# Decoder layer on one core: the w_down product in two halves of 1024 columns, with seven block products for 8 of the 22 pairs of k tiles in each

## What is computed

```
h = rmsnorm(x, g_ffn_pre[l])
ff = (jax.nn.silu(h @ w_gate[l]) * (h @ w_up[l])) @ w_down[l]
x = x + rmsnorm(ff, g_ffn_post[l])
```

## Time and profile before

| | |
|---|---|
| time, median of 3 runs | 1215.16 us (1214.73 to 1216.29) |
| the profiled execution's own time | 1216.34 us |
| its span, first to last instruction | 1214.6 us |
| mean granted TensorE clock | 0.998 |
| PE busy | 1202.1 us, 99% |
| DVE, ACT, POOL busy | 857.3, 651.6, 153.6 us |
| chain that ended last | PE 94%, DMA 3%, DVE 2%, ACT 1% |
| loads of w_down | 44 of 1 MB |

### The profile page before, as it was taken

The page is one execution under the profiler, slowest core; times in us unless marked ns, Lnnn a source line. Parts: engine busy times, 40 slices in busy tenths (PEclk is TensorE's granted clock), DMA queues, the critical chain, the costliest instruction groups (busy, mean ns, idle before and its releaser), DMA issues.

```text
span 1214.6 us, 16282 instructions
## 1 busy us (share of the span) xinstructions
PE 1202.1 (99%) x5812; PEld 1007.3 (83%) x5812; DVE 857.3 (71%) x1107; ACT 651.6 (54%) x860; POOL 153.6 (13%) x122
## 2 busy tenths in 40 slices
PE   8999999999999999999999999999999999999997
PEld 7888888888888888888888888888888888888886
DVE  6657877877776755777888888788888744444444
ACT  5654666474564745655555555555555544343432
POOL 2000200000000000004333323432332100000000
PEclk9999999999999999999999999999999999999999
DMA  8656867767686555464566556566555755555651
GB/s 314 210 148 159 208 152 160 176 138 209 159 198 189 193 206 180 168 193 155 206 208 207 189 184 216 172 207 207 197 187 187 259 207 181 201 192 189 205 176 69
DMA packets 121842, 229.60 MB, mean 189 GB/s; under 512 B 7360, under 2 KB 24000, under 8 KB 121280
## 3 DMA queue, kind: packets, MB, share of 16 engines
q1 hardware_dynamic: 121504, 226.85, 60.1%
q0 software_dynamic: 288, 2.10, 0.4%
HBM read 226.83 MB, written 2.10 MB: 188 GB/s over the span
## 4 chain that ended last, share of the span: by engine, by line
PE 94%; DMA 3%; DVE 2%; ACT 1%; issue 0%; SPq 0%; DVEq 0%; ACTq 0%
PE bank L1580 92%; DMA raw<-in_w_in 2%; PE bank L1878 1%; DMA resid<-in_x 1%; DVE w_lo L1002 1%; ACT w_hi L603 0%; PE bank L1585 0%; PE bank L1794 0%; DVE h L1029 0%; DVE resid L1344 0%; PE bank L1851 0%; DVE hT L1015 0%; DVE gT L1229 0%; ACT L771 0%; DVE ff_out L1337 0%
## 5 line engine op out<-in xcount | busy, mean ns | idle before, releaser
L1580 PE MATMUL bank<-w_hi,h2T 128*128 128x512 f32 x1126 | 359.4, 390 | 0.0
L1002 DVE TENSOR_TENSOR w_lo<-raw,w_hi 128x1024 fp32r<-128x1024 f32 x172 | 209.3, 1223 | 129.9 <-ACT w_hi L603 129.3
L603 ACT ACTIVATE w_hi<-raw 128x1024 fp32r<-128x1024 f32 x172 | 180.6, 1059 | 174.3 <-PE bank L1580 159.4
L1580 PE MATMUL bank<-hT,w_hi 128*128 128x512 f32 x768 | 271.7, 397 | 0.0
L1580 PEld LDWEIGHTS bank<-w_hi,h2T 128*128 128x128 f32 x1126 | 211.3, 188 | 44.0
L1580 PE MATMUL bank<-w_hi,ffT 128*128 128x512 f32 x704 | 217.2, 389 | 0.0
L1580 PE MATMUL bank<-hT,w_lo 128*128 128x256 f32 x768 | 214.6, 279 | 0.0
L1580 PE MATMUL bank<-w_lo,h2T 128*128 128x512 f32 x543 | 211.4, 389 | 0.0
L1544 DVE TENSOR_TENSOR w_lo<-raw,w_hi 128x1024 fp32r<-128x1024 f32 x88 | 107.9, 1226 | 121.3 <-ACT w_hi L963 121.3
L1481 DVE TENSOR_TENSOR w_lo<-raw,w_hi 128x1024 fp32r<-128x1024 f32 x116 | 148.3, 1285 | 47.6 <-ACT w_hi L927 47.3
L1580 PEld LDWEIGHTS bank<-hT,w_hi 128*128 128x128 f32 x768 | 144.0, 187 | 32.4
(11 more groups left out here) (212 smaller groups left out, 1217.4 us busy)
## 6 DMA issues: line engine op xcount, KB each, us to landing
raw<-in_w_in SPq DMA_DIRECT2D x63, 1024.0 KB, 10.0
raw<-in_w_down SPq DMA_DIRECT2D x44, 1024.0 KB, 5.0
raw<-in_w_up SPq DMA_DIRECT2D x80, 512.0 KB, 4.0
raw<-in_w_gate SPq DMA_DIRECT2D x80, 512.0 KB, 4.8
raw<-in_w_out SPq DMA_DIRECT2D x16, 1024.0 KB, 5.0
raw<-in_w_gate SPq DMA_DIRECT2D x4, 1024.0 KB, 5.2
raw<-in_w_up SPq DMA_DIRECT2D x4, 1024.0 KB, 6.4
resid<-in_x SPq DMA_DIRECT2D x2, 1024.0 KB, 7.2
```

The source lines that it names most:

```text
L603: act.activation(part_of(w_hi, rnd, s), src, ACT.Copy).then_inc(hi_done, 1)
L1002: dve.tensor_tensor(part_of(w_lo, rnd, s), raw_sub(rnd, s)[1], part_of(w_hi, rnd, s).bitcast(F32), ALU.subtract).then_inc(lo_done, 1)
L1580: return pe.matmul(out_, lhsT, rhs, start=start, stop=stop, skip_group_check=True)
```

## The change

**w_down by halves.** Columns 0 to 1023 are one group, 1024 to 2047 another. In each, 22 units of two k tiles, a chunk of 512 + 512 columns of w_down, loaded as two transfers of 512 KB with the code of the gate and up groups. `DOWN` gives the kinds: units 2, 4, ... 16 by seven products, the others regular, so S and R units alternate and five R units stand at the end. `unit_hi`, `unit_lo`, `weight_sums`, `partial_sums`, `up_sums` and `gate_sums` are used for both kinds of group. The half's sums go to `down_part`, from which squares and gains are taken; `ff_out` shrinks to the first half's columns. In the second half the last eight pieces are reordered so that the first 512 columns are complete before the last four pieces, which are done tile by tile as before.

**Sums of ff pair by pair.** The tokens' block sums of ffT (`token_sums`) are made for each S unit anew, 16 times: POOL adds hi and lo (128 x 512) and makes four sums of 128 x 128, between its first and its second difference of that unit; behind the unit's second piece ACT rounds them (128 x 512) and DVE makes their rest (128 x 512) into `d_ops`, which has two places. PE waits for that (`d_ready`) before the unit's first piece.

The core of the diff:

```diff
 FINAL = Plan("RRSRSRRR")
+DOWN = Plan("RRSRSRSRSRSRSRSRSRRRRR")
+LAST_HALF = Plan(DOWN.units)
+LAST_HALF.pieces[-8:] = [(n, piece) for piece in range(2) for n in range(18, 22)]
+DOWN_SEVEN = [n for n in range(KF // 2) if DOWN.units[n] == "S"]
 DOWN_FIRST = FF_FIRST + (FF_GROUPS - 2) * FULL.subs + FINAL.subs
-R_DOWN = R_FF + 2 * FF_GROUPS
-DOWN_SUBS = KF // 2
-N_SUBS = DOWN_FIRST + 4 * DOWN_SUBS
+N_SUBS = DOWN_FIRST + 2 * DOWN.subs
...
+def chunk_of(i, n):
+
+    return (n if down_half(i) is None else KF // 2 * down_half(i) + n) % 4
...
-        ff_out = sb("ff_out", [P, TT, D], stack=last)
+        ff_out = sb("ff_out", [P, TT, D // 2], stack=last)
         g_post2 = sb("g_post2", [P, D], stack=last)
+        down_part = sb("down_part", [P, 4, 512], stack=last)
+        d_ops = sb("d_ops", [P, 2, 2, 4, P], F32R, stack=last)
+        d_whole = sb("d_whole", [P, 2, SEQ], stack=last)
+        d_sum = sb("d_sum", [P, 4, P], stack=last)
...
-            for n in range(4 * KF // 4):
-                g, k = divmod(n, KF // 4)
-                load(R_DOWN + n // 4, n % 4, rows(w_down, 4 * k, 4, 512 * g, 512),
-                     counted=DOWN_FIRST + 8 * (n // 4))
+            ends = [ff_base(FF_GROUPS - 1) + FINAL.base[n + 1] for n in range(4, 8)]
+            for half, (up_col, gate_col) in enumerate(((512, 0), (1024, 1536))):
+                i = FF_GROUPS + half
+                ends += [ff_base(i) + DOWN.base[n + 1] for n in range(KF // 2)]
+                for n in range(KF // 2):
+                    unit_rows(i, n, ends[KF // 2 * half + n], ((w_down, up_col), (w_down, gate_col)))
...
+            def weight_sums(i, n, plan, between=None):
+
+                q, made = chunk_of(i, n), sums_index(i, n)
+                b12, b22, b11, b21 = (raw[:, q, 512 * c:512 * (c + 1)] for c in range(4))
+                pool.wait_ge(raw_up[q], up_arrived(i, n))
                 pool.tensor_tensor(b12, b22, b12, ALU.subtract).then_inc(t3_ready, 1)
-                pool.wait_ge(t2_ready, 3 * i + (j - 2))
+                if between:
+                    between()
+                pool.wait_ge(t2_ready, made + 1)
                 pool.tensor_tensor(b22, b22, b11, ALU.subtract).then_inc(t14_ready, 1)
-                pool.wait_ge(lo_done, ff_base(i) + (FULL.base[n] + 2))
+                pool.wait_ge(lo_done, ff_base(i) + (plan.base[n] + 2))
                 pool.tensor_tensor(b21, b21, b11, ALU.subtract).then_inc(t14_ready, 1)
...
+            def token_sums(d, n):
+
+                a11, a21 = d_whole[:, 0, 0:P], d_whole[:, 0, P:SEQ]
+                a12, a22 = d_whole[:, 1, 0:P], d_whole[:, 1, P:SEQ]
+                if d:
+                    pool.wait_ge(d_step, 5 * d)
+                    pool.wait_ge(d_ready, d)
+                pool.tensor_tensor(d_whole[:], ffT[:, 2 * n:2 * n + 2, 0:SEQ].bitcast(F32),
+                                   ffT[:, 2 * n:2 * n + 2, SEQ:2 * SEQ].bitcast(F32), ALU.add).then_inc(d_step, 1)
+                pool.wait_ge(d_step, 5 * d + 1)
+                pool.tensor_tensor(d_sum[:, 0], a21, a22, ALU.add).then_inc(d_step, 1)
+                pool.tensor_tensor(d_sum[:, 2], a11, a21, ALU.subtract).then_inc(d_step, 1)
+                pool.wait_ge(d_step, 5 * d + 2)
+                pool.tensor_tensor(d_sum[:, 1], d_sum[:, 0], a11, ALU.subtract).then_inc(d_step, 1)
+                pool.wait_ge(d_step, 5 * d + 4)
+                pool.tensor_tensor(d_sum[:, 3], a12, d_sum[:, 1], ALU.subtract).then_inc(d_step, 1)
+
+            pool.wait_ge(ff_lo, 2 * FF_GROUPS - 2)
+            for half in range(2):
+                for c, n in enumerate(DOWN_SEVEN):
+                    d = len(DOWN_SEVEN) * half + c
+                    weight_sums(FF_GROUPS + half, n, DOWN, between=lambda: token_sums(d, n))
...
+                    if plan.units[n] == "S" and piece == 1:
+                        d = len(DOWN_SEVEN) * half + DOWN_SEVEN.index(n)
+                        act.wait_ge(d_step, 5 * d + 5)
+                        act.activation(d_ops[:, d % 2, 0], d_sum[:], ACT.Copy).then_inc(d_rounded, 1)
...
+                    if plan.units[n] == "S" and piece == 1:
+                        d = len(DOWN_SEVEN) * half + DOWN_SEVEN.index(n)
+                        dve.wait_ge(d_rounded, d + 1)
+                        dve.tensor_tensor(d_ops[:, d % 2, 1], d_sum[:], d_ops[:, d % 2, 0].bitcast(F32),
+                                          ALU.subtract).then_inc(d_ready, 1)
...
+                    if m in (6, 8) and half == 1:
+                        if m == 6:
                             dve.wait_ge(post_in, 32)
-                        emptied(2 + g % 2, ff_out, g_post2, g, Q_POST2)
+                        gained(i - 1, m // 8, m // 8)
+                    if half == 1 and m == plan.subs - 4:
+                        partial_sums(i, DOWN, 4)
+
...
+                if t == 0:
+                    dve.wait_ge(tile_full, 2)
+                else:
+                    dve.wait_ge(sub_done, N_SUBS)
+                gate_sum_of(FF_GROUPS + 1, t, 0)
+                dve.wait_ge(sq_done, Q_POST2 + TT * 3 + t + 1)
+                link(dve.tensor_tensor(down_part[:, 2 * t, :], down_part[:, 2 * t, :], g_post2[:, 1536:D], ALU.mult))
...
+                if half is None:
+                    j = SEVEN.index(n)
+                    s1, s2, s3, s4 = ((s_upper(j)[:, c, :], s_lower(j)[c // 2][:, c % 2, :]) for c in range(4))
+                else:
+                    d = len(DOWN_SEVEN) * half + DOWN_SEVEN.index(n)
+                    s1, s2, s3, s4 = ((d_ops[:, d % 2, 0, c, :], d_ops[:, d % 2, 1, c, :]) for c in range(4))
+                    if piece == 0:
+                        pe.wait_ge(d_ready, d + 1)
+                pe.wait_ge(lo_done, ff_base(i) + (m + 1))
+                if first and piece == 2:
+                    pe.wait_ge(ff_lo, 2 * i if half != 1 else 2 * FF_GROUPS)
+                pair = (((c0 + 2, s4, False), (s0 + 2, tokens(0, 0), first)), ((c0, tokens(0, 1), False),),
+                        ((s0, s3, first), (s0 + 3, s2, first)),
+                        ((s0 + 1, s1, first), (c0 + 1, tokens(1, 1), False)))[piece]
+                for c, (b, operand, new_) in enumerate(pair):
+                    ins = products(b, *operand, slot, c, new_)
+                ins.then_inc(sub_done, 1)
...
-            pe.wait_ge(part_done, 2 * FF_GROUPS - 2)
-            for g in range(4):
-                pe.wait_ge(acc_free, E_DOWN + g + 1)
-                for s in range(DOWN_SUBS if g < 3 else DOWN_SUBS - AHEAD):
-                    n = DOWN_SUBS * g + s
-                    if g == 0:
-                        pe.wait_ge(ff_lo, s + 1)
-                    sub_tokens(DOWN_FIRST + n + 1, down_slot(n), ffT, 2 + g % 2, 2 * s, KF - 1)
-                    if g == 0 and s == 1:
-                        turned_ff(FF_GROUPS - 1, 0)
-            last_subs(DOWN_FIRST + 3 * DOWN_SUBS, DOWN_SUBS - AHEAD, DOWN_SUBS, ffT, 3)
+            def down_group(half, plan):
+
+                i, odd = FF_GROUPS + half, half == 0
+                c0, s0 = sum_banks(odd)
+                pe.wait_ge(part_done, 2 * i - 2)
+                for m in range(plan.subs - 4 * half):
+                    n, piece = plan.pieces[m]
+                    if plan.units[n] == "R":
+                        if n == KF // 2 - 4:
+                            pe.wait_ge(ff_lo, 2 * FF_GROUPS)
+                        sub_tokens(ff_base(i) + (m + 1), ff_slot(i, odd, m), ffT, c0 // 2 + 1 - piece, 2 * n, KF - 1)
+                        if m == 2 and half == 0:
+                            turned_ff(i - 1, s0)
+                    else:
+                        if n == DOWN_SEVEN[0] and piece == 0:
+                            pe.wait_ge(gate_sum, 2 * i - 2)
+                        seven_piece(i, odd, plan, m, c0, s0)
+
+            down_group(0, DOWN)
+            down_group(1, LAST_HALF)
```

More of the change, by code:

```diff
@@ L260, in hybrid_layer, with parts, ff @@
         ctx.callback(ffn.close)
-        def ff(t):
-            return part[:, 2 * t + 1, :]
+        def parts(i):
+            return part if down_half(i) is None else down_part
+        def ff(t, i=0):
+            return parts(i)[:, 2 * t + 1, :]
         def s_upper(j):
@@ L334, in hybrid_layer @@
         s_summed = sem("s_summed")
+        d_step = sem("d_step")
+        d_rounded = sem("d_rounded")
+        d_ready = sem("d_ready")
         s_rounded = sem("s_rounded")
@@ L932, in first_product @@
                 act.wait_ge(sub_done, ff_base(i) + plan.after_seven)
-                act.activation(part[:, 0, :], bank[:, s0 + 2, :], ACT.Copy).then_inc(p1_out, 1)
+                act.activation(parts(i)[:, 0, :], bank[:, s0 + 2, :], ACT.Copy).then_inc(p1_out, 1)
             def ff_group(i, odd, plan=FULL, first=False):
@@ L955, in _ @@
             ff_group(FF_GROUPS - 1, False, FINAL)
[L958 to L973, removed]
@@ L974, in _, with square_dump @@
-            for g in range(4):
[L975 to L978, removed]
```

(40 more changed lines are left out.)

210 lines of the change are left out of this document (115 added, 95 removed).

## The result

| | before | changed |
|---|---|---|
| median | 1215.13 us (4 runs, 1214.73 to 1216.29) | 1243.62 us (4 runs, 1243.03 to 1248.17) |
| ratio | 1 | 1.0232 [1.0213, 1.0251] |
| the profiled execution: time, span | 1216.34, 1214.6 us | 1243.03, 1241.3 us |
| mean granted TensorE clock | 0.998 | 0.999 |

A forecast was written before the change was run, and what follows sets the result against it. The prediction took the turn shared by DVE and POOL in the w_down stage as the bound: -10.9 + 51.8 + 1.0 + 2.4 + 0.7 = +45.0 us on the median 1215.2 gives 1260 us, range 1240 to 1284.

The forecast's parts named there:

- the full turn: w_down stage: DVE's and POOL's SBUF operations, served one after the other, set the pace; 1251 to 1281 us, chance 0.74.
- Matmuls removed: w_down stage: 16 S units save 3 matmuls each, 48 x 0.2267 = -10.9 us, if PE is fed.
- The turn's first signs in the gate groups: Gate groups: ACT waits 20.8 us for POOL's L577, PE loses 3.0 us to a late `w_lo`.
- DVE and POOL take turns: S and R units: DVE operations with two SBUF inputs and POOL's are served one after the other, 10.45 us per pair.
- The length of a step, 13.9: w_down, S unit to S unit: 13.9 us against PE's 10.20, 3.7 us of waits in fourteen steps, +51.8 us.
- First S unit +1: First half of w_down: the first S unit's pieces come 0.3 to 1.5 us late, priced +1 us.
- gain products +2.4: Second half of w_down: the first half's four gain products stand among the S units, 4 x 0.61 = +2.4 us.
- The end, +0.7: Kernel's end: the last result needs DVE's addition from PSUM before ACT's square, +0.7 us.
- Priced at nothing: w_down stage: partial sums, ACT's rounding of token sums, loads and added waits were taken to add nothing to the sum.
- B, PE fed: Rival, w_down stage: PE stays fed if the turn is below 10.9 us a step; 1205 us, chance 0.08.
- C, half of it: Rival, w_down steps: POOL's short operations slip in beside DVE's or the ring covers more; 1233 us, chance 0.10.
- D: Rival, w_down steps: the chain of waits from POOL's dependent sums adds to the turn; 16.9 us a step, about 1300, chance 0.08.

## Why the prediction was right, and where its size was off

It named the sign, the mechanism and the place. Its forecast of 1260 was 16.4 us over the 1243.62 measured, which lies inside its range. But its lowest case for the full turn, 13.4 us a step and 1251 us, was above what came: the time is inside only because the range reached down to 1240. By its steps:

- **Matmuls removed, -10.9.** Right: 5764 for 5812, at the distance of before.
- **The turn's first signs in the gate groups.** One of them was misread: the 3.0 us for a late `w_lo` in the earlier trace rows are the idle time of PEld, the weight loads. PE itself lost nothing there; it was busy for 264.98 of 265.00 us. The sum doesn't use it.
- **DVE and POOL take turns.** Right, and shown: with fills in place of POOL's reads the step is 10.9, with the sums running unhooked it is unchanged.
- **The length of a step, 13.9, measured 12.93.** This is the term of the sum that was mis-sized. Two of its parts are measured by themselves. The step without POOL's sums, 10.45 + 0.61 = 11.06, is 10.90: 0.16 too much. POOL's sums, 1.24 + 1.6 = 2.84, are 2.03: 0.81 too much. In the turn a 512-column operation holds 2.27 - 1.14 = 1.13 and not 1.24, and a short one 1.42 - 1.14 = 0.28 and not 0.4, as the chain of the changed kernel shows in steady alternation (start, us, what):

```profile
1010.39 1.42 POOL d_sum L643
```

  By these holds the five sums would be 2.25, 0.2 more than the 2.03. Most of that is at the last sum, L645, which meets a short DVE operation: from DVE's sum L1570 to its next operation it is 0.76 us (1011.51 to 1012.27), and 0.61 in the kernel with the sums made once, so only 0.15 is added. The start of an operation, which I had added to each of them, seems to lie beside DVE's operation: 0.28 and less are held, where a short one alone takes 0.46. So PE waits 2.73 a step and not 3.7: 14 x 0.97 = 13.6 of the 16.4 us.
- **First S unit +1, gain products +2.4.** Together 38.7 - 14 x 2.73 = 0.5 us where 3.4 was forecast. The first S unit does lose 0.61 and 0.58 us, at 979.49 and 981.72, and the gains do stand in the turn (two operations of 0.61 take 3.49):

```profile
1109.66 3.49 DVE L1629 TENSOR_TENSOR ff_out<-down_part,g_post 128x512 f32<-128x512 f32 x2
```

  I had counted both on top of full steps. PE's timeline shows otherwise. From the first matmul with `d_ops` of one S unit to that of the next, the first step is 12.43 us in the first half (976.67 to 989.10) and 13.14 in the second (1109.88 to 1123.02), and each of the other twelve is 12.93 to 12.95. So the first S unit's loss lies inside a first step that is 0.5 shorter than the others. The second half's first step, which has the four gain products, is 0.7 longer than the first half's, where 2.4 was priced. That PE starts these steps with four pieces ready in the ring is my explanation; no run tests it.
- **The end, +0.7.** Right: 0.74, also with all units regular. In DVE's timeline:

```profile
1233.19 0.69 DVE L1509 TENSOR_TENSOR down_part<-down_part,bank 128x512 f32<-128x512 f32 x1 [0.23 <-PE bank L1692]
```

- **Priced at nothing: partial sums, ACT's rounding, smaller loads, the added waits.** Right. The loads: the stage is 240.06 with all units regular. The added waits: the unhooked sums. The partial sums: PE waits for nothing from 1066.72 to 1113, which covers the start of the second half. The rounding: DVE stands for it once, for 0.2 us.
- **Rivals.** B, PE fed: its condition, a step of 10.9 as the point of break-even, was met by the two kernels without POOL's reads, and they broke even. With two R units to an S unit and POOL held back PE is fed, and the kernel is 6.2 us faster, with 36 matmuls removed that are worth 8.2. C, half of it: 14 x 2.73 = 38.2 of the 51.8 showed, because short operations take their turn but hold it shortly, not because they slip in beside DVE's. D: excluded, by the unhooked sums.

The rule cited there from the Trainium skill (SBUF — State Buffer, Who interferes with whom), that the loser is blocked for the whole instruction, agrees with the short operations here: 1.32 to 1.44 us for 128 columns beside a 1024-column operation of DVE, against 0.46 where DVE reads a PSUM bank, as here in POOL's timeline:

```profile
1094.24 0.46 POOL L641 TENSOR_TENSOR d_sum<-d_whole 128x128 f32<-128x128 f32 x1
```

That 0.46 is near the 0.41 I estimated from GPSIMD Engine Reference, section Elementwise — side-by-side cycle accounting, and the estimate of 0.28 from its 2.6 cycles for each element alone is the most that such an operation holds of the turn (0.15 to 0.28).

## What to carry to other kernels

- Where DVE operations with two SBUF inputs meet POOL operations that read SBUF, add the two per step and compare the sum with PE's step; busy shares of 80% and 28% of the span can hide a full resource. Only work that both shares can pay for is worth moving off PE: here an S unit in place of an R unit saves PE 0.68 us, and the step's turn goes from 4 x 1.14 = 4.6 to 12.9 us.
- Such work pays if it is spread until the sum is below PE's step, and if POOL is held until DVE has made what PE needs next. That turned +28 us into -6, with 12 of the 16 S units. The sum below PE's step gave -3, the hold the rest.
- A long wait (ACT's 50.8 us) beside a full resource doesn't show the cause: here the stage stayed the same when the wait was taken away and the work left in place.

## What was new about the hardware

- POOL operations with 128 columns cost DVE 0.15 to 0.28 us each beside it, less than the 0.46 they last alone. Four of them cost 2.03 - 1.13 = 0.9 us a step, less than one of 512 columns (1.13). That what overlaps is their start is inferred from these numbers.
- POOL's fills of 128 x 512 take 0.53 us each, and DVE's 1.14 beside them is untouched.
- While both had work, the two engines alternated one operation each, however unequal: in the step shown eight POOL operations lie between DVE's eight, a 128-column one for a 1024-column one.
